# Gathers of the first tile moved ahead of the barrier between two layers

## The reference

```python
x = x + gt_a * (mix @ w_out)
h = rms_norm(x, g_norm_ffn) * (1 + sc_f) + sh_f
hid = silu(einsum('nd,edf->nef', h, w_gate)) * einsum('nd,edf->nef', h, w_up)
hid = hid * gate[:, :, None]            # two of 16 experts per row are not zero
x = x + gt_f * einsum('nef,efd->nd', hid, w_down)
# next layer
h = rms_norm(x, g_norm_mix) * (1 + sc_a) + sh_a
proj = h @ w_in
```

## Time and profile before

| | us |
|---|---|
| runs of the kernel: median (lowest to highest of 3) | 1460.44 (1457.29 to 1461.26) |
| the profiled execution | 1458.88 |
| its span, first to last instruction | 1457.0 |
| busy in it: PE | 1235.0 (85%) |
| DVE | 564.8 (39%) |
| ACT | 368.7 (25%) |
| POOL | 152.2 (10%) |

### The profile page before, as it was taken

How to read it: one execution, slowest core, us unless ns; L and a number is a source line. 1 busy time by engine, 2 the same in 40 slices (tenths; PEclk the granted TensorE clock), 3 DMA queues, 4 the chain that set the end, 5 groups by cost and what they waited for, 6 DMA issues and landing times.

```text
span 1457.0 us, 16000 instructions
## 1 busy us (share of the span) xinstructions
PE 1235.0 (85%) x6139; PEld 719.1 (49%) x6139; DVE 564.8 (39%) x1458; ACT 368.7 (25%) x861; POOL 152.2 (10%) x218
## 2 busy tenths in 40 slices
PE   4898799977889869999837988998786995999990
PEld 0452254543545456777524533544354454777770
DVE  1227689123236531111107268970423453211115
ACT  2224120035741111111115142001468111111111
POOL 0312050010000150000020114110100011000002
PEclk7899799997999969999968999899758996999995
DMA  9428997260860479999952220225030026699985
GB/s 363 129 81 300 366 329 229 82 226 4 312 228 29 145 259 360 361 365 369 315 193 103 63 66 29 73 67 156 6 79 2 0 87 223 219 368 369 362 298 209
DMA packets 137174, 284.98 MB, mean 196 GB/s; under 512 B 11613, under 2 KB 91909, under 8 KB 130697
## 3 DMA queue, kind: packets, MB, share of 16 engines
q1 hardware_dynamic: 116416, 209.70, 42.7%
q0 software_dynamic: 8352, 42.50, 8.4%
q10 hardware_dynamic: 12329, 31.74, 6.1%
HBM read 237.91 MB, written 52.40 MB: 199 GB/s over the span
## 4 chain that ended last, share of the span: by engine, by line
PE 69%; DVE 12%; DMA 6%; ACT 6%; issue 3%; SPq 2%; ACTq 1%; POOL 1%; POOLq 0%; DVEq 0%
PE ps L508 45%; PE ps L813 9%; PE ps L518 6%; PE ps L671 3%; PE ps L732 3%; ACT arena L1177 2%; SPq L418 2%; DMA X<-in_x_sample 2%; DVE arena L1481 2%; DVE small L1480 1%; DVE arena L1520 1%; DVE arena L1571 1%; PE ps L632 1%; DMA arena<-y_d,sid 1%; DMA W<-in_w_gate 1%
## 5 line engine op out<-in xcount | busy, mean ns | idle before, releaser
L508 PE MATMUL ps<-W,arena 128*128 128x256 f32 (+1 forms) x1280 | 347.2, 427 | 9.2 <-DMA W<-in_w_gate 3.4
L508 PEld LDWEIGHTS ps<-W,arena 128*128 128x128 f32 x1280 | 241.9, 193 | 84.3 <-issue 53.5
L508 PE MATMUL ps<-W,hT 128*128 128x512 f32 (+3 forms) x480 | 194.1, 562 | 10.2 <-DVE gt L1352 7.1
L518 PE MATMUL ps<-C,arena 128*128 128x128 f32 (+3 forms) x851 | 124.4, 288 | 80.5 <-DVE arena L1400 18.2
L518 PEld LDWEIGHTS ps<-C,arena 128*128 128x128 f32 (+3 forms) x851 | 100.5, 152 | 121.7 <-issue 36.3
L813 PE MATMUL ps<-W,hT 128*128 128x512 f32 (+1 forms) x320 | 144.8, 607 | 5.7 <-ACT hT L1234 5.7
L508 PEld LDWEIGHTS ps<-W,hT 128*128 128x128 f32 (+1 forms) x480 | 87.2, 186 | 110.2 <-issue 82.7
L508 PE MATMUL ps<-hT,W 128*128 128x128 f32 (+1 forms) x512 | 129.3, 414 | 7.1 <-ACT arena L1101 7.1
L508 PEld LDWEIGHTS ps<-hT,W 128*128 128x128 f32 x512 | 79.0, 193 | 58.3 <-issue 50.5
L1783 DVE TENSOR_TENSOR arena<-arena,ps 128x256 f32<-128x256 f32 x32 | 13.5, 421 | 216.0 <-ACT arena L1275 216.0
L813 PEld LDWEIGHTS ps<-W,hT 128*128 128x128 f32 (+1 forms) x320 | 57.1, 183 | 80.2 <-issue 73.8
(11 more groups left out here) (244 smaller groups left out, 1124.1 us busy)
## 6 DMA issues: line engine op xcount, KB each, us to landing
W<-in_w_ada SPq DMA_DIRECT2D x48, 1024.0 KB, 7.9
W<-in_w_gate SPq DMA_DIRECT2D x32, 1024.0 KB, 10.4
W<-in_w_up SPq DMA_DIRECT2D x32, 1024.0 KB, 12.8
W<-in_w_down SPq DMA_DIRECT2D x32, 1024.0 KB, 7.4
arena<-x_d SPq DMA_DIRECT2D x33, 512.0 KB, 11.5
y_d<-arena ACTq DMA_DIRECT2D x33, 512.0 KB, 7.3
W<-in_w_in SPq DMA_DIRECT2D x16, 1024.0 KB, 7.8
arena<-arena SPq DMA_DIRECT2D x128, 79.2 KB, 2.1
```

Source lines behind the costliest of these rows:

```text
L508: ins = T.matmul(out, l, r, start=n == 0, stop=n == len(pairs) - 1, skip_group_check=True)
L518: count(T.transpose(o, i, ident[0:m, 0:m]), done if n == len(outs_ins) - 1 else None)
```

## The change

GpSimd's gathers become a function of the tile. The waits for the stores and the two gathers of tile 0 now stand ahead of `leave`, the eight gathers of tiles 1 to 4 behind it. It is so for both layers, since the loop body is one.

```diff
                 pool.wait_ge(L["jdone"], 1)
-                leave(pool, "pool")
                 for b in range(2):
                     pool.wait_ge(s_yst[b], (l + 1) * STORED)
-                for t in range(NT):
+                gather(0)
+                leave(pool, "pool")
+                for t in range(1, NT):
+                    gather(t)
```

More of the change, by code:

```diff
@@ L1898, in _ @@
                             scatter(t, k, sid2, s_xo[l])
-                pool.wait_ge(L["jdone"], 1)
-                leave(pool, "pool")
-                for b in range(2):
-                    pool.wait_ge(s_yst[b], (l + 1) * STORED)
-                for t in range(NT):
+                def gather(t):
                     m = rows_of(t)
@@ L1908, in _ @@
                                              ).then_inc(s_yg[t], 16)
+                pool.wait_ge(L["jdone"], 1)
+                for b in range(2):
+                    pool.wait_ge(s_yst[b], (l + 1) * STORED)
+                gather(0)
+                leave(pool, "pool")
+                for t in range(1, NT):
+                    gather(t)
 _INS = ["x_prompt", "x_sample", "c_prompt", "c_sample", "cache_k", "cache_v", "cache_idx_k", "state_conv",
```

## The result

The changed kernel takes 1467.53 us (median of 8 runs, 1462.62 to 1471.91), the kernel before 1458.42 in the same comparison (1454.47 to 1462.16): a ratio of 1.0057, 95% interval 1.0039 to 1.0074, so 8.3 us more (5.7 to 10.8). The forecast was slower by 5.2 us.

What follows compares the result with a forecast made beforehand. TensorE (69%) bounds the kernel, so only the joint and the end matter. Tail +4.9 and joint +0.3 give +5.2 us: 1464.1 for the profiled execution, 1465.6 against the median; forecast's chance 60%, range 1461.2 to 1468.5.

Steps and rivals of the forecast that it cites:

- longer at the joint: Rival (13%): gathers moved into the w_in rush need 8.3 us after their record; joint +2.6, time 1468.
- What bounds: TensorE (69%) overall; the change matters only at the layer joint and kernel end, where the joint's chain goes through tile 1.
- The drain waits for the landing: Barrier in both places: a GpSimd drain waits until its gathers have landed, plus 0.45 us.
- works but doesn't wait: Rival (16%): the drain costs 82 ns per DMA behind the gathers; joint -0.9, tail +2.1, time 1461.6.
- Not slower: Rival (7%): the drain neither waits for the gathers' data nor adds to them; joint -4.1, tail +0.3, time 1456.6.
- Plus 0.45 us: Drain's end after its last gather landed, read from the end-of-block drain: 0.45 us.
- the old clean-up of 62 DMAs would end at about 754.3 and lies beneath it: Joint: the drain's per-DMA work is hidden by the wait for landing, which ends the drain at 755.9; joint +0.3 us.
- The tail, +4.9 us: Kernel end: drain ends at 1434.17, tile 1's gathers start at 1435.97 and land at 1442.48, not 1437.47.
- Nothing catches up since DVE paces the rest: Tail: DVE goes on at 3.7 us per tile, so tile 1's delay stays to the end.
- Others let go later, at no cost: Joint: the other engines are let go some 4.6 us later; tile 0's work still ends about 763, ahead of tile 1.
- That cover would be gone with a barrier some 3 us later still: Joint: a barrier some 3 us later than forecast would no longer leave tile 0's work hidden ahead of tile 1.
- 0.8 us from wait to first gather at the joint: Joint: GpSimd needs 0.8 us from seeing the last job done (746.13) to its first gather.

Runs made afterwards that it cites:

- the early drain: Changed kernel plus one more GpSimd drain just before its wait for the last expert job, where it idles: 1.0053 of the kernel before.
- new_order_no_drain: Changed kernel with GpSimd arriving at the barrier by a plain semaphore increment, with no drain: 0.9953 of the kernel before.

## Why the prediction was right, and where its sizes were off

- **The size as a whole.** The forecast was +5.2 us with +6 as the end of its own range; measured are +8.3 (5.7 to 10.8). That way and mechanism were right is shown below. That the time fell within the stated range, which went up to 1468.5, is owed to the rival "longer at the joint", whose +2.6 and +4.9 us come nearest to the measured time. Its cause isn't what happened: it put tile 0's landing about 11.4 us after the last job, and it came at 10.0. That its +2.6 at the joint is near the measured +2.7 is luck.
- **What bounds.** Right. From tile 1 at the joint to the last job of layer 1 it is 656.3 us before and 655.9 after, so what moved is joint and tail. At the joint the chain stayed on tile 1; in the tail it is tile 1's delay and then tile 3's. The 4.05 us that DVE idles after tile 0 is the clearest sign that the moved gathers were not the ones waited for.
- **The drain waits for the landing.** Right; it was read from the one drain at the end of the block. With the early drain two DMAs are left for the barrier's drain, and it takes 9.34 us and ends 0.12 us after their landing; by the rival "works but doesn't wait" it would take 0.2. "Not slower" falls too: the changed kernel's drain outlasts the second gather's record by 5.1 us in the tail and by 10.1 at the joint.
- **Plus 0.45 us.** This term was mis-sized. It was 0.04 us and 41 ns for each of ten DMAs, and not a constant: with 20 DMAs it is 0.86 us in the tail, with 64 it is 2.66 at the joint.
- **"the old clean-up of 62 DMAs would end at about 754.3 and lies beneath it".** This is the sentence that failed. Half of the clean-up comes behind the landing. It is 2.2 of the 2.4 us by which the joint came out above the forecast's +0.3; tile 0's later landing (10.0 us after the last job, I took 9.4) is another 0.6, and tile 1 took 8.4 us from start to landing and not 8.96, which gave 0.6 back. The rest is that the sum at 8.96 came to +0.6 and I took +0.3.
- **The tail, +4.9 us.** It is +6.9. The drain ended 0.4 us later behind the landing than I took, tile 1 took 7.2 us and not 6.5 from its first gather to landing (its second gather took 1.36 us where the others take 0.95), which makes +6.0; the last 0.9 is tile 3, which landed 7.9 us after its second gather's record and not 6.6. "Nothing catches up since DVE paces the rest" held; that something falls back further I had not looked for. Stores of the output run beside the last gathers in both kernels (the first is issued at 1438.84 before and at 1443.37 after), so their presence alone isn't new. What made tile 3 late was not tried and stays open.
- **Others let go later, at no cost.** Right: ScalarE scales tile 0 at 15.0 us after the last job and DVE has combined it at 20.0, 4 us ahead of tile 1. "That cover would be gone with a barrier some 3 us later still" didn't hold: the barrier was 2.8 us later than forecast, and the cover stayed, since tile 1's gathers stand behind the same barrier and came later with it.
- **0.8 us from wait to first gather at the joint.** It was 0.29 us, half a us in the kernel's favour.
- **The Trainium skill's rule** ("VectorE: DVE Perf Modes", "The DRAIN you can't avoid": pre- and postamble DRAINs of about 12 ns on all engines). The section speaks of the runtime's own drains, and those of the barrier are the program's. GpSimd's drain comes near this order, 40 to 53 ns, when nothing was issued since the last one. Carried over to a GpSimd drain behind DMAs, 12 ns would be wrong by up to 12.6 us here.

## What to carry to other kernels

Where an engine that issues DMAs drains, ask two things: what is in flight at that moment, and how many DMAs it has issued since it last drained. Work moved ahead of a barrier is only early for those who can use it before the barrier opens; here nobody could, and everybody waited for its data. The gain lay next door: a drain in idle time, or none, takes the old joint from 21.3 to 16 us and the kernel to 0.9966 and 0.9962 of its time. Only without the drain does the new order lose nothing (0.9953); its 1.5 us at the joint are seen in the trace and are too small for the time to show. A drain is left out only where nothing behind the barrier relies on it.

## What the hardware showed that was not expected

- A GpSimd drain costs 82 ns for each DMA issued since the last drain even when the last of them landed 190 us ago or more: 5.13 us for 62, 2.34 for 28, 0.04 to 0.05 for none.
- If it must wait for a landing, only 41 ns per DMA remain behind it, as far as 64 DMAs (2.66 us); with 92 it is 3.0 us and not 3.8.
- A plain increment from GpSimd opened the barrier 1.1 us after the last job, with the gathers ahead of it still running: in the new order ScalarE's table load follows 1.1 us after the last job (744.07 against 742.95 in new_order_no_drain; GpSimd's second gather starts at 744.53).
